# Differential attention on one core: dense pieces in 9 groups per step, mostly four between scores and transposes, in place of 14 smaller groups

## The reference, cut to what matters

```python
q, k, v, g = jnp.split(h @ w_in, [A_WIDTH, 2 * A_WIDTH, 3 * A_WIDTH], axis=-1)
...
s = jnp.einsum('bqhmd,bkhmd->bhmqk', qb, keys).astype(f32) * ATTN_SCALE
p = jax.nn.softmax(s, axis=-1)
a = p[:, :, 0] - lam * p[:, :, 1]
return jnp.einsum('bhqk,bkhe->bqhe', a.astype(vals.dtype), vals)
...
o = rms_norm_2(o, subln_g, SUBLN_EPS) * (1.0 - lam_init)
return o.reshape(o.shape[:2] + (A_WIDTH,)) * jax.nn.silu(g)
```

## Time and profile before

| | before |
|---|---|
| median of three runs | 1821.35 us |
| lowest, highest | 1820.37, 1825.03 us |
| the profiled execution's own time | 1821.82 us |
| its span, first to last instruction | 1820.0 us |
| mean granted clock of TensorE, share of 2.4 GHz | 0.941 |
| TensorE matmuls busy | 1602.4 us (88% of the span) |
| VectorE, ScalarE, GpSimd busy | 977.7, 748.6, 495.1 us |
| the seven steps with dense pieces, from the first scores | 932.5 to 1324.6 us |

### The profile page before, as it was taken

One profiled execution on the slowest core, in us unless ns is written; L12 is line 12 of the kernel. 1 busy time (PEld: TensorE's weight loads), 2 busy tenths in 40 slices (PEclk: granted clock), 3 DMA queues, 4 the chain that ended last, 5 costly groups with the idle time before them and its releaser, 6 DMA issues.

```text
span 1820.0 us, 22915 instructions
## 1 busy us (share of the span) xinstructions
PE 1602.4 (88%) x7904; PEld 1202.8 (66%) x7904; DVE 977.7 (54%) x2217; ACT 748.6 (41%) x1376; POOL 495.1 (27%) x209
## 2 busy tenths in 40 slices
PE   7999898889599999996499999999968799978877
PEld 6876565568378888884377777777737568744445
DVE  7146553282787767677744455444552374156633
ACT  6227665423432323233434445444452332246642
POOL 4542222233145445443021111112102223400002
PEclk9999999999699999998699999999988889979998
DMA  6831111262244555553011111101101122200001
GB/s 195 176 120 36 65 58 53 92 231 93 74 148 160 174 171 173 163 173 116 18 52 35 35 35 46 35 35 42 33 18 35 58 71 70 81 24 1 1 12 58
DMA packets 47345, 148.59 MB, mean 82 GB/s; under 512 B 5766, under 2 KB 8070, under 8 KB 47144
## 3 DMA queue, kind: packets, MB, share of 16 engines
q1 hardware_dynamic: 36328, 112.45, 19.8%
q10 hardware_dynamic: 10944, 35.20, 6.0%
HBM read 141.01 MB, written 6.62 MB: 81 GB/s over the span
## 4 chain that ended last, share of the span: by engine, by line
PE 56%; DVE 11%; issue 4%; ACT 3%; DVEq 1%; ACTq 0%
PE ps L311 29%; PE ps L315 14%; PE ps L1067 3%; PE ps L1103 2%; PE ps L482 2%; PE ps L512 2%; PE ps L501 2%; DVE b_sb L600 1%; DVE xn L1685 1%; DVE sqsum L359 1%; DVE x2l L1677 1%; DVE ropea L1704 1%; PE ps L1079 1%; DVE b_sb L637 1%; PE ps L363 0%
## 5 line engine op out<-in xcount | busy, mean ns | idle before, releaser
L871 POOL TENSOR_TENSOR w_l<-raw,w_h 128x1024 fp32r<-128x1024 f32 (+1 forms) x189 | 475.0, 2514 | 1137.1 <-ACT w_h L296 1137.1
L296 ACT ACTIVATE w_h<-raw 128x1024 fp32r<-128x1024 f32 x189 | 199.7, 1058 | 500.4 <-PE ps L311 448.2
L311 PE MATMUL ps<-x2h,w_h 128*128 128x512 f32 x832 | 248.8, 368 | 47.0 <-DVE x2l L1677 21.5
L311 PE MATMUL ps<-x1h,w_h 128*128 128x512 f32 x584 | 241.5, 414 | 30.8 <-POOL w_l L871 19.4
L311 PE MATMUL ps<-x2h,w_l 128*128 128x512 f32 x832 | 234.6, 351 | 0.0
L315 PE MATMUL ps<-x2l,w_h 128*128 128x512 f32 x832 | 233.9, 350 | 0.0
L311 PE MATMUL ps<-x1h,w_l 128*128 128x512 f32 x584 | 233.5, 400 | 0.0
L315 PE MATMUL ps<-x1l,w_h 128*128 128x512 f32 x584 | 232.9, 399 | 0.0
L311 PEld LDWEIGHTS ps<-x2h,w_h 128*128 128x128 f32 x832 | 134.6, 191 | 93.9 <-issue 48.2
L1637 DVE CUSTOM_DVE_ANT_0 terms<-mraw,crow 128x1024 f32<-128x1024 f32 x96 | 179.3, 1868 | 2.7 <-issue 0.3
L311 PEld LDWEIGHTS ps<-x1h,w_h 128*128 128x128 f32 x584 | 113.2, 194 | 59.2 <-issue 20.1
(11 more groups left out here) (256 smaller groups left out, 2371.3 us busy)
## 6 DMA issues: line engine op xcount, KB each, us to landing
raw<-in_w_mlp SPq DMA_DIRECT2D x64, 512.0 KB, 3.5
mraw<-in_w_mod ACTq DMA_DIRECT2D x51, 512.0 KB, 4.0
raw<-in_w_a SPq DMA_DIRECT2D x32, 512.0 KB, 3.4
raw<-in_w_att SPq DMA_DIRECT2D x25, 512.0 KB, 11.1
raw<-in_w_b SPq DMA_DIRECT2D x20, 512.0 KB, 3.4
raw<-in_w_g SPq DMA_DIRECT2D x16, 512.0 KB, 3.5
gates<-g_stage ACTq DMA_DIRECT2D x16, 256.0 KB, 2.0
raw<-in_w_up SPq DMA_DIRECT2D x8, 512.0 KB, 4.5
```

The lines of the kernel that those rows point to most:

```text
L296: nc.scalar.activation(split(u)[0], raw[:, u % RAW], ACT.Copy).then_inc(w_hi, 1)
L311: mm = nc.tensor.matmul(o, w[:, k], xh(k), start=(first and k == k0 and wi == 0), stop=(last and k == k1 - 1 and wi == 1))
L871: nc.gpsimd.tensor_tensor(l[:, ks], raw[:, u % RAW, ks], h[:, ks].bitcast(F32), ALU.subtract).then_inc(w_lo, 1)
```

## The change

In TensorE's stream the 32 dense pieces of a step are dealt out in other groups; in ScalarE's stream the copy of v (`take` j = 2) moves one tile earlier. No instruction is added or removed. The whole diff:

```diff
--- before.py
+++ after.py
@@ -1082,7 +1082,7 @@
 
                 wait_head(pe, "ro", head, 2, 2)
                 scores(0)
-                dense(2)
+                dense(4)
                 wait_head(pe, "v", head, 1, 1)
                 wait_head(pe, "ln", head, 1, 0)
                 for b in range(6):
@@ -1092,23 +1092,21 @@
                 dense(4)
                 for qt in range(4):
                     scores(qt + 2)
-                    dense(2)
+                    dense(4)
                     turns(qt)
-                    dense(1 + qt % 2)
+                dense(2)
                 turns(4)
-                dense(2)
                 wait_head(pe, "m", head, 12, 12)
                 wait_head(pe, "te", head, 6, 4)
                 for b in range(6):
                     mm = nc.tensor.matmul(ps[:, 6], a_v[:, b, :], a_pt[:, b, :], start=(b == 0), stop=(b == 5))
-                dense(2)
                 turns(5)
                 dense(2)
                 wait_head(pe, "te", head, 6, 6)
                 for b in range(2):
                     mm = nc.tensor.matmul(ps[:, 7, 0:C], a_v[:, 4 + b, :], a_pt2[:, b, :], start=(b == 0), stop=(b == 1))
                 mm.then_inc(ha["pv"], 1)
-                dense(6)
+                dense(4)
                 wait_head(pe, "sq", head, 1, 1)
                 nc.tensor.matmul(ps[:, 4], ones[:], a_sq[:, 0:S], start=True, stop=True)
                 nc.tensor.matmul(ps[:, 5, 0:C], ones[:], a_sq[:, S:SC], start=True, stop=True).then_inc(ha["st"], 1)
@@ -1329,7 +1327,7 @@
                         if qt == 2 and more:
                             take((i, c + 1), 1, True)
                         exps(qt + 2, 1)
-                    if qt == 5 and more:
+                    if qt == 4 and more:
                         take((i, c + 1), 2, True)
                     turned(qt)
                 wait_head(act, "pv", head, 1, 1)
```

## The result

The changed kernel takes 1833.95 us (median of 10 runs, 1827.44 to 1839.58) against 1820.47 us of the kernel before in the same comparison (10 runs, 1815.61 to 1825.03): 1.0072 of the time, 95% interval 1.0058 to 1.0087. It is slower by 13.5 us, where 9.0 were forecast; 1833.95 lies in the range of 1823 to 1844, between the forecast (1830.3) and the rival in which the clock falls (from 1837).

What follows compares the result with a forecast made beforehand. TensorE was taken to bound the seven steps with dense pieces; -0.03 (groups) - 2.75 (old waits) + 4.07 (new waits) = +1.29 us a step, +9.0 in all, giving 1830.3 us, range 1823 to 1844.

Steps and rivals of the forecast that it cites:

- the rival in which the clock falls: TensorE's clock drops to 1.2 GHz in the new waits, 4 to 10 falls, 1837 to 1847 us; chance 0.25.
- Bound: TensorE bounds each of the seven steps with dense pieces: matmuls busy 53.79 of 55.90 us.
- Groups without waits: TensorE's regrouped matmuls, start to start: joining groups is worth nothing, -0.03 us a step, ends -0.5 and +0.5.
- The prediction's own sign: Prediction is wrong if joints between TensorE's groups change a step's busy time by more than 0.5 us.
- Waits that go: TensorE's waits for q (0.49), k (0.43), the combine of tile 4 (0.87) and v (0.96) vanish: 2.75 us a step.
- Waits that come: TensorE waits 2.03 us at piece 17 for the copy of k, 2.04 at piece 25 for that of v.
- The sum: Per step -0.03 - 2.75 + 4.07 = +1.29 us; seven steps +9.0 us, giving 1830.3 us.
- The prediction's two cases: New waits at unchanged clock, 1830.3 us, chance 0.57; clock falling in those waits, middle 1840 us, chance 0.25.
- The no-change case: New TensorE waits about as long as the old, wait for k near 0.7 us: 1821.35 us; chance 0.11.
- The faster case: Copies reach pieces 17 and 25 in time: 1816 us with one wait hidden, 1802 with both; chance 0.07.
- a move of the last step: Prediction is wrong if the last step, without dense pieces, or anything outside the seven steps moves.

Runs made afterwards that it cites:

- The experiment with the old joints: Kernel with copies of k and v both early, dense pieces at tiles 0 and 2 split 3 and 1 around the transposes again: 1803.73 us, ratio 0.9914.
- the experiment at ratio 1.0004: Changed kernel with the copy of k moved behind turned(1) but ahead of exps(4, 0) on ScalarE: 1821.57 us.
- the ScalarE edit alone: Kernel before with only the copy of v moved ahead of turned(4), TensorE's groups as before: 1834.41 us, ratio 1.0070.

## Why the prediction was right, and the term that was missed

**Bound.** Right: TensorE bounds the steps, and only its own waits and its clock moved their time. VectorE and ScalarE got other idle times; they count only through the two chains.

**Groups without waits** (-0.03 us a step). Right to about 0.15: a step without a fall is 1.02 us longer than 55.92; its new waits are 2.64 - 0.63 and 2.50 - 0.57, together 3.94, the old 2.75 are gone, and what is left is -0.17. The experiment with the old joints shows the same for two of them directly. The prediction's own sign, a change of busy time by more than 0.5 us, is at its edge: 53.3 against 53.8. But two waits in place of four account for 0.33 of it: a wait from start to start is longer than the idle time, and the difference counts as busy (2.75 - 2.11 = 0.64 before, 3.94 - 3.63 = 0.31 now).

**Waits that go** (2.75). Right: none of the four is in the profile after.

**Waits that come** (2.03 and 2.04). Right in place, cause and size: 2.01 and 1.93. The second is 0.11 shorter than forecast, nearly all of it because ScalarE started the copy of v 0.71 us behind the copy ahead of it and not 0.81. Removing the first by its cause gave 55.01 us a step, both 53.62, against 54.9 and 53.6 worked out by the same prices.

**The sum.** Waits alone: forecast +1.29 a step and +9.0 us, measured +1.02 and +7.2. The measured +13.5 has a second term, and here the prediction's step failed that set the clock aside. It gave the falls a chance of 0.25; its reason against them was that "here full-width matmuls stand on both sides, there half-width ones". That is no protection. It is not quite what stands there either: the 1.4 us ahead of the wait for k are transposes and scores of 64 rows. Five of the 14 new waits of the profiled run were followed by a fall of 1.6 us, all five at piece 17. The rival's "4 to 10 falls" took in these five, but its sum of the waits was 1.8 us too high and its base 0.9 (1821.35 against 1820.47), so its 1837 was missed by 3 us. The prediction's two cases are one: the waits cost 7.2 us, and filling one of them removed nearly all of the remaining 6.3. That the forecast came within 4 us of the measured time is in part luck: its waits were too dear by 1.8 us and its falls stood at nothing. The range held by its width: the ends for the waits alone reached 1838.5, while the waits alone came to about 1827.7 (1820.47 + 7.2).

How many falls the unprofiled runs had can't be read; 6.3 / 1.6 makes about four, if all of the rest is falls in the steps. That is worked out, not seen. The runs' spread (1827.44 to 1839.58) says little on it, since the kernel before, with no fall in its steps, spreads by 9.4 us too. The profiled run, at 1839.58, is the slowest of the ten.

The trace of the kernel before held more on this than the prediction used. In the second attention the two stretches of the earlier trace rows are single idle stretches, 1.79 us with a fall behind it and 1.71 without, and a third one came 6 us later, with a fall (clock 1.00 in the 4 us before 1752, 0.69 in the 4 us behind):

```profile
1752.76 1.29 PE L501 MATMUL ps<-ident,b_sb 128*128 128x128 f32 x8 [2.59 <-DVE b_sb L637]
```

The forecast idle time was 1.9 us for k and 1.7 for v. Read by length alone, these three point to falls at piece 17 and none at piece 25, which is what came.

**No change and faster.** The no-change case asked for a copy of k ahead of the exponential: that is the experiment at ratio 1.0004. The faster case put 1802 on both copies in time: that version gave 1805, with 0.34 us of idle time left per step. The reasons against both, that the pieces stand behind the border and ScalarE's order forbids it, hold for the kernel as changed.

**Outside the steps.** In the profiled run the time ahead of the steps is 0.6 us longer and that behind them 2.1 us. The edit touches neither, and the profiles of the other kernels spread there by 928.5 to 935.4 us and 489.6 to 498.6 us. Still, by the prediction's words a move of the last step is a sign of being wrong, and it did move, by 1.25 us. In the profiles of all nine kernels with the new TensorE order the last step takes 34.3 to 36.2 us to its last matmuls, with the old order 33.86 (before) and 32.62 (the ScalarE edit alone). The instructions of that step are the same and the clock falls in it in both kernels, at other places. With one profile for each kernel it stays open whether the change causes this.

## What to carry to other kernels

Before filler work (independent work that covers a wait, here the dense pieces) is moved between two dependent groups, look at what the filler's own first piece waits for: here the pieces that were to cover a chain stood behind a border that needed the end of that chain, and four longer covers turned into two longer waits. The buffer's copy then has to move on its engine ahead of whatever depends on the work in front of the border; with that done the same regrouping gave 0.8%. Part of that may be had from early copies in the old order, which was not run. Count the clock too: an idle stretch of 1.94 us on TensorE, followed by a fall of 1.6, cost nearly twice its length.

## What the runs showed of the hardware that was not expected

- A single idle stretch of TensorE, with dense matmuls running at full clock up to at most 1.4 us ahead of it (transposes and short scores lie between; ahead of the 2.21 us nothing does), can be followed by a fall of the clock from 2.4 to 1.2 GHz. Steps with a fall are 1.4 to 1.6 us longer than steps without in the same kernel. By the length of the idle stretch, with the number of steps that have a fall behind it, in the seven steps of this case's profiles: 0.72 to 0.88 us (for the combine of tile 4, before) 0 of 7; 1.06 us 0 of 7; 1.69 us 0 of 35 (five kernels); 1.94 to 2.08 us 9 of 14; 2.21 us 3 of 7; 2.42 us 5 of 7; 2.43 to 2.57 us 3 of 7.
- Among the lengths with falls, more idle time did not bring more of them (1.94: 9 of 14, 2.43: 3 of 7), though the counts are small. What decides in a given step is left open; with the same instructions and the same idle time one step has a fall and the next has none.
- The Trainium skill (TensorE: Matmul & The Clock Gate, A second HAM failure mode: psum-queue depth-cycling) says that micro-idle stretches between groups let the clock oscillate. In the seven steps the traces agree for stretches from 1.94 us on, and not for the shorter ones above.
